# Cross attention of a hybrid encoder: query and output projections as three products of split operands

## The reference, cut to what matters

```python
def _cross_attention(h, mem_k, mem_v, w_xq, w_xo):
    q = (h @ w_xq).reshape(b, t, XATTN_HEADS, XATTN_HEAD_DIM)
    s = jnp.einsum('bqhd,bkhd->bhqk', q, mem_k).astype(jnp.float32) * XATTN_HEAD_DIM ** -0.5
    p = jax.nn.softmax(s, axis=-1)
    o = jnp.einsum('bhqk,bkhd->bqhd', p.astype(mem_v.dtype), mem_v).reshape(b, t, XATTN_W)
    return o @ w_xo

x = x + _rmsnorm(y, norm_mix_post)
x = x + _rmsnorm(_cross_attention(_rmsnorm(x, norm_x_pre), mem_k, mem_v, w_xq, w_xo), norm_x_post)
x = x + _rmsnorm(_swiglu(_rmsnorm(x, norm_ffn_pre), w_ffn_in, w_ffn_out), norm_ffn_post)
```

## Time and profile before

| | |
|---|---|
| median of 3 runs | 2890.88 us (2887.85 to 2892.25) |
| profiled execution, span | 2887.4 us |
| TensorE (PE) busy | 2757.3 us, 95% |
| VectorE (DVE) busy | 1620.5 us, 56% |
| ScalarE (ACT) busy | 745.3 us, 26% |
| mean granted TensorE clock over the span | 0.989 |
| DMA | 290.26 MB, mean 101 GB/s |

### The profile page before, as it was taken

One profiled execution on the slowest core, in us unless ns is written; L12 is line 12 of the kernel. 1 busy time (PEld: TensorE's weight loads), 2 busy tenths in 40 slices (PEclk: granted clock), 3 DMA queues, 4 the chain that ended last, 5 costly groups with the idle time before them and its releaser, 6 DMA issues.

```text
span 2887.4 us, 63061 instructions
## 1 busy us (share of the span) xinstructions
PE 2757.3 (95%) x26472; PEld 2574.4 (89%) x26472; DVE 1620.5 (56%) x2991; ACT 745.3 (26%) x1779; POOL 243.9 (8%) x423
## 2 busy tenths in 40 slices
PE   7999999999999989999989999999999999999998
PEld 6877889999999789999988778899999997899997
DVE  5444655666664266664374455556666633766633
ACT  1143443222232330000112433432223324200001
POOL 1221112000000100000002211110000000000000
PEclk9999999999999999999999999999999999999999
DMA  4453436222263133323225434452223532223231
GB/s 136 129 144 103 143 104 169 72 72 64 74 175 103 44 92 88 88 87 86 78 85 136 119 114 137 100 158 72 72 64 111 156 92 68 77 88 89 85 88 58
DMA packets 420762, 290.26 MB, mean 101 GB/s; under 512 B 38544, under 2 KB 386352, under 8 KB 420352
## 3 DMA queue, kind: packets, MB, share of 16 engines
q1 hardware_dynamic: 398496, 228.64, 28.8%
q0 software_dynamic: 21984, 57.59, 6.3%
HBM read 232.12 MB, written 54.07 MB: 99 GB/s over the span
## 4 chain that ended last, share of the span: by engine, by line
PE 80%; DVE 8%; ACT 3%; DVEq 3%; DMA 3%; issue 2%; ACTq 0%; SPq 0%
PE PS L740 35%; PE PS L809 9%; PE PS L1112 8%; PE PS L1045 7%; PE PS L718 4%; PE PS L1256 2%; DMA U<-gate_scratch 2%; ACT U L1371 1%; PE PS L855 1%; PE PS L1086 1%; ACT U L1374 1%; PE PS L759 1%; PE PS L1176 1%; PE PS L891 1%; PE PS L970 1%
## 5 line engine op out<-in xcount | busy, mean ns | idle before, releaser
L740 PE MATMUL PS<-U_r,WHI 128*128 128x272 f32 x2656 | 474.7, 289 | 11.3 <-DVEq L2283 7.5
L1374 ACT COPY U<-PS 128x272 f32<-128x272 f32 (+8 forms) x758 | 265.0, 374 | 747.0 <-PE PS L1112 140.0
L1858 DVE CAST WHI<-ring 128x1024 fp32r<-128x1024 f32 (+1 forms) x240 | 164.1, 684 | 472.8 <-PE PS L740 365.7
L740 PEld LDWEIGHTS PS<-U_r,WHI 128*128 128x128 f32 x2656 | 386.3, 188 | 16.8 <-DVEq L2283 11.7
L740 PE MATMUL PS<-brT_r,WHI 128*128 128x272 f32 x1728 | 357.4, 288 | 1.0 <-DVEq L1869 1.0
L740 PE MATMUL PS<-U_r,WLO 128*128 128x272 f32 x1696 | 350.3, 288 | 0.0
L740 PE MATMUL PS<-hT_r,WHI 128*128 128x272 f32 x1696 | 349.7, 288 | 0.0
L1868 DVE TENSOR_TENSOR WLO<-ring,WHI 128x1024 fp32r<-128x1024 f32 (+1 forms) x240 | 289.9, 1208 | 19.4 <-issue 1.3
L740 PE MATMUL PS<-brT_r,WLO 128*128 128x272 f32 x1344 | 278.2, 288 | 0.0
L809 PE MATMUL PS<-U_r,WHI 128*128 128x272 f32 x832 | 261.7, 314 | 12.4 <-ACT U L1374 12.3
L740 PEld LDWEIGHTS PS<-brT_r,WHI 128*128 128x128 f32 x1728 | 271.5, 188 | 1.9 <-DVEq L1869 1.9
(11 more groups left out here) (337 smaller groups left out, 4285.7 us busy)
## 6 DMA issues: line engine op xcount, KB each, us to landing
ring<-in_w_in_dram SPq DMA_DIRECT2D x126, 512.0 KB, 4.3
ring<-in_w_ffn_in_dram SPq DMA_DIRECT2D x88, 512.0 KB, 3.8
ring<-in_w_ffn_out_dram SPq DMA_DIRECT2D x32, 448.0 KB, 3.7
proj_scratch<-U POOLq DMA_DIRECT2D x104, 136.0 KB, 2.1
U<-proj_scratch SPq DMA_DIRECT2D x48, 272.0 KB, 4.3
ring<-in_w_branch_dram SPq DMA_DIRECT2D x48, 256.0 KB, 3.2
gate_scratch<-U POOLq DMA_DIRECT2D x88, 136.0 KB, 3.1
U<-gate_scratch SPq DMA_DIRECT2D x44, 272.0 KB, 2.9
```

What stands on the lines that cost most here:

```text
L740: ins = mm(PS[:, 2 * q + h, 0:HT], w, half(x, h), start=(first and k == 0 and n == 0), stop=(last and k == kn - 1 and n == len(terms) - 1))
L1374: return act.copy(out, in_)
L1858: copy(hi, src)
```

## The change

The units of w_xq and w_xo get places in the order of split units (V_XQ, V_XO), so that later units move up by 12 and the count of activation splits by 4. Query projection: VectorE calls `prenorm_split` (L1827) in place of `prenorm`, which makes the high part in a new view `XH` and the low part in place of `hT`, then splits the first two units; the others are split between tiles. TensorE calls `dense_split`, its first tile with `need`. Output projection: VectorE splits the first two units after the barrier, moves every head's values out of PSUM as a high part (cast) and a low part (subtraction), and then goes tile by tile: wait, split, add squares. The last two of these splits are the first two feed-forward units, which had their own lines before. SP's loads of w_xq and w_xo wait for splits instead of tiles.

```diff
-V_LATE, V_GATE, V_BR, V_OUT, V_FFI, V_FFO = 13, 39, 63, 87, 95, 139
+V_LATE, V_GATE, V_BR, V_OUT, V_XQ, V_XO, V_FFI, V_FFO = 13, 39, 63, 87, 95, 99, 107, 151
...
-X_SPLITS = 4 + 6 + 8
+X_SPLITS = 4 + 6 + 4 + 8
...
 def unit_of(v):
-    return v if v < V_FFI else v + U_FFI - V_FFI
+    return v if v < V_XQ else v + U_XQ - V_XQ
...
 def depth_of(v):
-    if V_BR <= v < V_OUT:
+    if V_BR <= v < V_OUT or V_XO <= v < V_FFI:
         return 4
...
+        XH = carver(2 * KM * T + T + 6 * T + 12 * T + KM * N_MEM)(KM, T, of=UR)
...
+        OXH = cv(X_HEADS, T, of=UR)
+        OXL = carver(KM * T + T + 2 * 512 * 4 + 2 * X_HEADS * N_MEM + X_HEADS * T)(X_HEADS, T, of=UR)
...
                 for j in range(4):
-                    unit("w_xq", 0, 8, P * j, tiles(G_XQ + j + 1))
+                    unit("w_xq", 0, 8, P * j, split(V_XQ + j))
                 for j in range(8):
-                    unit("w_xo", 0, 4, P * j, tiles(G_XO + j + 1))
+                    unit("w_xo", 0, 4, P * j, split(V_XO + j))
...
-                pe.wait_ge(h_ready, l * 24 + 16)
                 for n in range(N_XQ):
-                    dense(l, G_XQ + n, n % 4, U_XQ + n, 8, of_h, rot=3)
+                    dense_split(l, G_XQ + n, n % 4, V_XQ + n, lambda k: (XH[:, k, :], hTR[:, k, :]), rot=3,
+                                need=10 if n == 0 else None)
...
                 for n in range(N_XO):
-                    dense(l, G_XO + n, n % 3, U_XO + n, 4, lambda k, h: half(OX[:, k, :], h), rot=3)
+                    dense_split(l, G_XO + n, n % 3, V_XO + n, lambda k: (OXH[:, k, :], OXL[:, k, :]), rot=3)
...
-                dense_first(l, G_FFI, V_FFI, of_f, 10, sums=4)
+                dense_first(l, G_FFI, V_FFI, of_f, 14, sums=4)
...
-                prenorm(l, 2, "norm_x_pre")
+                prenorm_split(l, 2, "norm_x_pre", XH)
+                split_unit(l, V_XQ)
+                split_unit(l, V_XQ + 1)
                 for n in range(N_XQ):
                     tile(l, G_XQ + n)
+                    if n < N_XQ - 2:
+                        split_unit(l, V_XQ + n + 2)
                     ts(half(QX[:, n, :], 1), PS[:, 2 * (n % 4) + 1, 0:HT], X_DIM ** -0.5, None, ALU.mult) \
                         .then_inc(tile_freed_dve, 1)
                 phase_end(dve, l, 2)
+                split_unit(l, V_XO)
+                split_unit(l, V_XO + 1)
 
                 def x_evac(h):
                     dve.wait_ge(xa_out, l * 5 + h + 2)
-                    copy(OX[:, h, 0:SEQ], PS[:, x_bank(h), :]).then_inc(xa_evac, 1)
+                    take_high(OXH[:, h, 0:SEQ], PS[:, x_bank(h), :])
+                    dve.drain()
+                    tt(OXL[:, h, 0:SEQ], PS[:, x_bank(h), :], OXH[:, h, 0:SEQ].bitcast(F32), ALU.subtract) \
+                        .then_inc(xa_evac, 1)
...
-                        copy(OX[:, :, SEQ:T], PS[:, 7, 0:4 * DEC_SEQ].rearrange("p (h n) -> p h n", h=4)) \
-                            .then_inc(xa_evac, 1)
+                        rows = PS[:, 7, 0:4 * DEC_SEQ].rearrange("p (h n) -> p h n", h=4)
+                        take_high(OXH[:, :, SEQ:T], rows)
+                        dve.drain()
+                        tt(OXL[:, :, SEQ:T], rows, OXH[:, :, SEQ:T].bitcast(F32), ALU.subtract).then_inc(xa_evac, 1)
...
                 dve.sem_inc(tile_freed_dve, N_XO)
-                for a in range(1, KM - 2):
-                    add_square(l, 3, a)
-                split_unit(l, V_FFI)
-                split_unit(l, V_FFI + 1)
+                for n in range(N_XO):
+                    tile(l, G_XO + n)
+                    split_unit(l, V_XO + n + 2)
+                    if 1 <= n - 1 <= KM - 3:
+                        add_square(l, 3, n - 1)
```

## The result

The changed kernel takes 2898.82 us (median of 11 runs, 2891.5 to 2903.97) against 2890.13 (11 runs, 2887.85 to 2896.25): a ratio of 1.0023, 95% interval 1.0012 to 1.0033. It is slower by about 6.7 us by the ratio, 8.7 by the medians: a small difference, but its interval excludes 1. The profiled execution has a span of 2899.2 us, 11.8 more than that of before; it took 2900.97 us, 2.2 more than its kernel's median.

The account below looks back on a forecast made before the run. TensorE's issue rate was taken to bound the kernel wherever it does not wait. Per layer +3.9 (query stage) + 2.6 (evacuations) - 5.5 (output projection) = +1.0, +2.1 us over two layers: 2893.0 on the median, range 2887.0 to 2899.0.

Parts of the forecast that it names:

- the slower rival: Longer evacuations idle TensorE: half clock in layer 1's attention (+1.1) and at output projection starts (+3.6); 2897.7, chance 0.13.
- TensorE's work: Both projections: each becomes 192 matmuls in 24.1 us, saving 21.5 us over both projections and both layers.
- the rival with three quarters: Both projections: three products cost three quarters of the plain one, 22.0 us instead of 24.1; 2884.6, chance 0.02.
- The late start: Query projection: TensorE waits for prenorm_split and the first w_xq unit's split, 7.4 us per layer.
- The clock at the query projection: Query projection's start: eighteen matmuls at half clock after the wait, 1.8 us; bounds nothing or 2 us.
- The w_xo splits and the freeing of banks: First two w_xo splits (3.0 us) hidden in VectorE's idle time; banks freed 2.1 us later, nobody waits; cost nothing.
- The evacuations: Attention: moving each head out of PSUM as cast and subtraction costs 2.6 us per layer; bounds 0.8 to 3.4.
- The rival that they are absorbed: Attention: the loop is latency-bound, so only the last evacuation counts; -1.5 us, 2889.4, chance 0.11.
- The clock in the attention: Layer 0's attention: a half-clock stretch of 1.1 us that may come or go with any shift.
- The output projection: VectorE's splits fit beside 3.0 us tiles, TensorE runs through in 24.1 us; the stage gains 5.5 us per layer.
- rival 5: Change does not take effect as said, for instance TensorE waits at each tile for VectorE's splits; either size, chance 0.02.
- rivals 1 and 2: Clock does not fall before the query projection (0.07); evacuations absorbed except the last (0.11); each 2889.4, together -5.1.

Follow-up runs that it names:

- the filled kernel: The changed kernel plus 15 additional plain float32 products on TensorE in the wait ahead of the query projection; ratio 0.9996 to the kernel before.

## Why the forecast was right or wrong

The time of 2898.82 us lies inside the range, 0.2 us from its end. The likeliest case, no difference at 2893.0, did not come; what came is nearest to the slower rival: 2897.7 by its working, with chance 0.13. In the profile its terms came in kind and in other sizes. It had the two layers 6.8 us longer, and they are 11.7 us longer; the profiled execution itself, 2900.97 us, lies outside the range. That the median is inside, and 1.1 us from the rival's figure, is in part luck.

- **TensorE's work: right.** 24.1 us were forecast for 192 products; at full clock they take 24.1 to 24.4. The ratio of a plain to three split products is 1.22, as the rows had it; the rival with three quarters is out.
- **The late start: right**, 7.35 us against 7.4, and its two causes: the weight split behind the last pair gives back 3.6 us when it is moved.
- **The clock at the query projection: right in kind, too small in size.** This is one of the steps that failed. The sum took 18 slow products and 1.8 us from the feed-forward block's start. In the changed kernel's profile the first 24 take 5.5 us at half clock. Against the 24.4 us of the filled kernel it loses 2.5 us, outside the bound of 2 us that the text gave. Over the twelve unfilled starts of the six profiles the loss is 1.2 to 2.7 us, 2.0 on average, so that the 1.8 was low for this profile and near the usual.
- **The w_xo splits and the freeing of banks: right**, hidden.
- **The evacuations: right.** 2.6 us a layer forecast; 29.85 - 27.26 = 2.6 measured with the clock full. The rival that they are absorbed falls.
- **The clock in the attention: the step that failed most in the profile.** The forecast let a stretch of half clock of 1.1 us come or go in its range and put nothing into the sum. The changed kernel's profile has it in both layers and longer: 32.5 us against 29.85, 2.65 us a layer. How much of it the other runs have is open. The profiled execution is among the slower ones, with a mean clock of 0.984 against 0.9855 over all eleven.
- **The output projection: its tiles right, its start wrong.** Without gaps, as said; but 25.8 us for 24.1. The rival that had it was given 0.13, because its wait was far from the 5.63 us of the one case in the rows; that took the length of one wait for a measure. Waits of 1.55 us are enough in four cases of eight.

In sum, a layer was to be 1.05 us longer. By the profiled executions it is 5.3 and 6.4 us longer, and the terms without the clock give 7.35 - 5.0 + 2.6 - 5.25 = -0.3 us. All of the loss beyond that in these two profiles is TensorE at half clock: 2.5 + 2.65 + 1.5 us a layer, less the 1.1 us that layer 0 of before had lost too. For the median, 6.7 to 8.7 us longer and not 11.8, only the part at the query projection is shown by experiment: the kernel with the filled wait is even with before, in time and in mean clock. How the rest is shared between the attention and the output projection's start is not shown.

Two small things in the forecast's figures don't fit together. Its chances for no difference add up to 0.83 before any part of rival 5, and it says 0.82; for slower they add up to 0.14, and it says 0.13. And its range begins at 2887.0, while rivals 1 and 2 together, at -5.1, come to 2885.8.

The Trainium skill, TensorE: Matmul & The Clock Gate, section "A second HAM failure mode: psum-queue depth-cycling", describes short, frequent idle times between groups of matmuls that send the clock back and forth. The runs here fit that in kind. They put 1.55 us beside it, and an attention stage in which TensorE is busy 2.7 to 3.0 of 4 us and whose clock falls to half in 8 layers of 24.

## What to carry to other kernels

A product that is cheaper on TensorE pays only from the moment at which its operands are there: work out when the last of the new preparations ends, behind everything that is queued on its engine, and order them by what TensorE wants first. Add to each new wait of TensorE the products behind it at half clock. If the wait can't be removed, throwaway products in it can keep the clock up, and two half-length pieces of work in a latency-bound loop may fit where one long piece does not.

## What the runs showed of the hardware that was not expected

- A wait of 3.8 us costs as much clock as one of 7.35: 27.1 and 26.6 us for the query projection against 24.4 filled. Fifteen plain products with nothing to do with the result, 7.04 us long, took that loss away in both layers; the same held for 8 and for 4.
- With 1.55 us of idle time four output projections of eight started at half clock, with 0.78 us or less none of sixteen.
- The attention's slow stretch begins at one place, some 5 us behind the first scores, and is there or not from layer to layer. The stage takes 27.3 or 28.4 us with the copies, and 29.85, 31.0 or 32.5 us with the evacuations as the change makes them, each time for the same instructions. How busy TensorE is just ahead does not decide it: in the 4 us around the first scores it is busy 2.6 to 2.8 us in all 24 layers, in the 8 that fall and in the 16 that don't. The times scatter with the clock: the 11 runs of the changed kernel spread over 12.5 us, with mean clocks from 0.987 in the fastest to 0.983 in the slowest; which stretches make up that spread can't be read from the means. What decides the fall stays open; filling the gaps inside the attention was not tried.
- The half clock can begin inside the wait and reach far into the work behind it. In the changed kernel it begins 4.5 us ahead of the query projection and ends about 6 us behind its start; in layer 0 of the kernel with the query projection alone it ends about 3 us behind the start, and the loss is 1.2 us instead of 2.5.
